# Sixteen dense tokens moved from the dense expert products to gathered rows, with a new start of the program

## What is computed

```python
q = (xb @ w_q).reshape(tb, PEER_HEADS, 2, PEER_HALF)      # 8 heads, 2 halves of 128
sc = jnp.einsum('thjd,hjnd->thjn', q, sub_keys)           # 128 keys in each half
s_half, i_half = lax.top_k(sc, K)                         # K = 16
# 256 sums of pairs; the best 16 name 16 of 128*128 experts for each token and head
idx = jnp.take_along_axis(cand_idx, top_pos, axis=-1)
g = jax.nn.softmax(top_s, axis=-1)
h = jax.nn.gelu(jnp.einsum('td,thkd->thk', xb, u[idx]), approximate=False)
out = jnp.einsum('thk,thkd->td', g * h, v[idx])
```

## Time and profile before

| | us |
|---|---|
| median of 3 runs | 1390.19 (1388.97 to 1390.58) |
| the profiled execution | 1392.18 |
| its span, first to last instruction | 1390.4 |
| TensorE busy | 1367.2 (98%) |
| VectorE busy | 1056.4 (76%) |
| GpSimd busy | 599.5 (43%) |
| ScalarE busy | 438.4 (32%) |
| DMA, mean over the span | 336 GB/s |

### The profile page before, as it was taken

The page is one execution under the profiler, slowest core; times in us unless marked ns, Lnnn a source line. Parts: engine busy times, 40 slices in busy tenths (PEclk is TensorE's granted clock), DMA queues, the critical chain, the costliest instruction groups (busy, mean ns, idle before and its releaser), DMA issues.

```text
span 1390.4 us, 16195 instructions
## 1 busy us (share of the span) xinstructions
PE 1367.2 (98%) x5402; PEld 935.1 (67%) x5402; DVE 1056.4 (76%) x2365; ACT 438.4 (32%) x1219; POOL 599.5 (43%) x516
## 2 busy tenths in 40 slices
PE   7999999999999999999999999999999999999999
PEld 5656648567588888888899999995444444444443
DVE  4535445799899999998589899998768667766665
ACT  2533522444411111113677887882000000000000
POOL 0000001632855554442356655564667745544540
PEclk9999999999999999999999999999999999999999
DMA  8322334985999999996899999999999999999998
GB/s 308 138 108 111 121 125 183 362 314 196 403 389 411 409 352 374 342 350 234 299 377 407 385 398 395 389 382 402 388 410 409 410 409 409 409 409 409 410 409 311
DMA packets 121762, 467.68 MB, mean 336 GB/s; under 512 B 13776, under 2 KB 14160, under 8 KB 115152
## 3 DMA queue, kind: packets, MB, share of 16 engines
q0 software_dynamic: 73728, 268.47, 49.8%
q1 hardware_dynamic: 47664, 197.66, 36.8%
q10 hardware_dynamic: 288, 0.52, 0.1%
HBM read 462.67 MB, written 3.93 MB: 336 GB/s over the span
## 4 chain that ended last, share of the span: by engine, by line
PE 94%; DVE 3%; ACT 2%; issue 1%; DMA 0%; SPq 0%; ACTq 0%; DVEq 0%
PE BANKS L941 32%; PE BANKS L965 32%; PE BANKS L741 11%; PE BANKS L733 10%; PE BANKS L960 4%; PE BANKS L924 1%; PE BANKS L713 1%; PE BANKS L857 1%; PE BANKS L768 1%; PE BANKS L778 0%; DMA BIG<-w_in 0%; PE BANKS L829 0%; DVE NMX L1574 0%; ACT BIG L1122 0%; DVE UV L1638 0%
## 5 line engine op out<-in xcount | busy, mean ns | idle before, releaser
L1685 POOL DMA_INDIRECT UV<-u,IDX x152 | 174.1, 1145 | 398.8 <-DVE IDX L1513 261.2
L1685 POOL DMA_INDIRECT UV<-v,IDX x159 | 191.1, 1202 | 165.9 <-DVE UV L1638 91.3
L1643 DVE SCALAR_TENSOR_TENSOR X<-UV,HG,X 128x1024 f32<-128x1024 f32 x159 | 203.7, 1281 | 39.3 <-DMA UV<-v,IDX 37.1
L941 PE MATMUL BANKS<-T 128*128 128x256 f32 x1024 | 229.2, 379 | 0.0
L965 PE MATMUL BANKS<-T,BIG 128*128 128x512 f32 x512 | 225.2, 592 | 0.0
L965 PE MATMUL BANKS<-Y,BIG 128*128 128x512 f32 x512 | 225.1, 592 | 0.0
L941 PE MATMUL BANKS<-T,Y 128*128 128x256 f32 x992 | 221.9, 379 | 0.0
L1638 DVE SCALAR_TENSOR_TENSOR UV<-UV,Y 128x1024 f32<-128x1024 f32 x152 | 184.9, 1221 | 42.2 <-DMA UV<-u,IDX 40.8
L941 PEld LDWEIGHTS BANKS<-T 128*128 128x128 f32 x1024 | 192.0, 190 | 24.9 <-issue 0.2
L941 PEld LDWEIGHTS BANKS<-T,Y 128*128 128x128 f32 x992 | 186.0, 190 | 24.0
L965 PEld LDWEIGHTS BANKS<-Y,BIG 128*128 128x128 f32 x512 | 97.3, 190 | 122.5 <-issue 122.5
(11 more groups left out here) (258 smaller groups left out, 1222.2 us busy)
## 6 DMA issues: line engine op xcount, KB each, us to landing
T<-u_t SPq DMA_DIRECT2D x64, 512.0 KB
T<-v SPq DMA_DIRECT2D x64, 512.0 KB
Y<-v SPq DMA_DIRECT2D x64, 512.0 KB
Y<-u_t SPq DMA_DIRECT2D x62, 512.0 KB
BIG<-w_in SPq DMA_DIRECT2D x23, 1024.0 KB, 6.7
BIG<-w_q SPq DMA_DIRECT2D x16, 1024.0 KB, 7.4
BIG<-w_out SPq DMA_DIRECT2D x8, 1024.0 KB, 5.9
UV<-v,IDX POOLq DMA_INDIRECT x159
```

The source lines that it names most:

```text
L941: last = nc.tensor.matmul(PS[(i + 2) % 4][:, 0:HT], ub[:, c, :], T8[:, 1, c, :], start=(c == 0), stop=(c == KC - 1))
L1643: stt(xb, row, HG[:, n % 2, i % UNIT:i % UNIT + 1], xb, ALU.mult, ALU.add).then_inc(used, 1)
L1685: pool.indirect_dma_start(row_place(s), None, u if kind == "ru" else v, bass.IndirectOffsetOnAxis(IDX[:, b, c:c + 1], 0)).then_inc(row_in[ ...
```

## The change

16 of the 256 dense tokens (240 to 255 of them, `EXTRA = 16`, `FEW = 240`) no longer go through the dense products of u: `gl` moves 240 columns. Their u products are made from gathered rows, one row for each partition, where the partition stands for a token and a head (16 x 8 = 128) and the row for one of the 16 choices: 16 gathers of 512 KB and 16 VectorE steps `eu`. The steps `xi` find their indices, `ye` spreads their x over the partitions, and `eh` does the Gelu and turns the result; `oh` multiplies it into the maps of the last 4 groups, and `gm` copies there. Their v products stay dense.

The planner is set anew: the due time is 3.36 us for each `gl`, 13 more `ru` and `rv` rows stand in the first u stage (95), and in the second 134 of them and the 16 `eu` (150). 202 rows are left for the v stage; its products are as before.

At the start the loads of x come ahead of the first weights and in two parts instead of three, 12 products of ones by ones go ahead of the first weights' wait, the sum of squares stands before the fourth chunk instead of the fifth, and the step sizes are made in four strips of 32 output rows, which a product with a 0/1 table adds up.

```diff
+STRIP = 32
+EXTRA = P // PH
+FEW = HT - EXTRA
+FEWG = FEW // NTOK
+WARM = 12
...
-            work += [item] + rows(3 - (n >= 13))
+            work += [item] + rows(3)
...
-    work += [first] + on("sel", 0) + rows(9) + on("oh", 0) + [second] + rows(3) + on("oh", 1) + [sums, keys, columns]
-    work += rows(1) + on("ws", 3)
+    work += on("xi", 0) + rows(1) + [first] + on("xi", 1) + on("sel", 0) + rows(9) + on("oh", 0) + [second] + rows(3) + on("oh", 1) + [sums, keys, columns]
+    work += rows(5) + on("ws", 3)
...
-        while w < len(work) and spent < 3.44 * (j + 1):
+        o += on("ye", (j - 4) // 2) if j in (4, 6) else []
+        while w < len(work) and spent < 3.36 * (j + 1):
...
     o += work[w:]
+    o += on("ye", 2)
...
+        o += on("eh", 2) if k == 57 else []
...
-        o += rows(1 + (k % 4 == 0))
+        o += rows(1 + (k % 4 == 0) - (k % 6 == 5))
+        o += extra(1) if k % 3 == 0 and k >= 3 else []
+        if k in (52, 54):
+            o += on("eh", (k - 52) // 2)
...
+            sp.dma_start(T8[:, 0, 0:4], x_t[:, 0, 0:4]).then_inc(ld_t_lower, 16)
             sp.dma_start(COLS[:], cols).then_inc(ld_cols, 16)
-            sp.dma_start(T8[:, 0, 0:2], x_t[:, 0, 0:2]).then_inc(ld_t_first, 16)
+            sp.dma_start(T8[:, 0, 4:8], x_t[:, 0, 4:8]).then_inc(ld_t_upper, 16)
             sp.dma_start(W[:, 0, 0:2 * HALF], tiles[0][0][:, 0:2 * HALF]).then_inc(w_first, 16)
-            sp.dma_start(T8[:, 0, 2:4], x_t[:, 0, 2:4]).then_inc(ld_t[0], 16)
-            sp.dma_start(T8[:, 0, 4:8], x_t[:, 0, 4:8]).then_inc(ld_t_upper, 16)
...
+                pe.wait_ge(ones_set, 1)
+                for k in range(WARM):
+                    nc.tensor.matmul(PS[7][:, 0:P], ONES, ONES, start=True, stop=True)
                 pe.wait_ge(w_first, 16)
-                for c0 in (0, 4):
-                    if c0:
+                for c0, c1 in ((0, 3), (3, 4), (4, KC)):
+                    if c0 == 3:
                         scale_map(0)
...
-                            last = nc.tensor.matmul(bank[0:NH, half * HT:(half + 1) * HT], WDT[:, c * NH:(c + 1) * NH],
-                                                    T8[:, half, c, :], start=(c == 0), stop=(c == KC - 1))
+                            strip = c % 4 * STRIP
+                            last = nc.tensor.matmul(bank[strip:strip + STRIP, half * HT:(half + 1) * HT],
+                                                    WDT[:, c * STRIP:(c + 1) * STRIP], T8[:, half, c, :],
+                                                    start=(c < 4), stop=(c >= 4))
...
-                        last = nc.tensor.matmul(PS[(i + 2) % 4][:, 0:HT], ub[:, c, :], T8[:, 1, c, :],
+                        last = nc.tensor.matmul(PS[(i + 2) % 4][:, 0:FEW], ub[:, c, :], T8[:, 1, c, 0:FEW],
                                                 start=(c == 0), stop=(c == KC - 1))
                     last.then_inc(hd_full, 1)
+                elif step == "ye" and i == 1:
+                    pe.wait_ge(ey_in, 1)
+                    for c in range(KC):
+                        last = nc.tensor.matmul(PS[5 + c // 4][:, c % 4 * P:(c % 4 + 1) * P], X[:, HB, c * P:(c + 1) * P], IDENT,
+                                                start=True, stop=True)
+                    last.then_inc(ye_full, 1)
+                elif step == "xi" and i == 0:
+                    pe.wait_ge(xi_in, 2)
+                    nc.tensor.matmul(PS[7][:, 0:P], ETOK, EALL, start=True, stop=True)\
+                        .then_inc(xi_full, 1)
...
+            def extra_rows(first):
+                if first:
...
+                    stt(EALL, ISELS[:, 1, 1, :], float(NKEY), ISELS[:, 1, 0, :], ALU.mult, ALU.add).then_inc(xi_in, 1)
+                    return
+                dve.wait_ge(xi_full, 1)
+                link(tt(EOWN.rearrange("p (k h) -> p k h", h=PH), PS[7][:, 0:P].rearrange("p (h k) -> p k h", k=TOPK),
+                        bc(OF_HEAD, 1, TOPK), ALU.mult))
+                link(nc.vector.reduce_sum(EIDXF, EOWN.rearrange("p (k h) -> p k h", h=PH), AXX))
+                nc.vector.tensor_copy(EIDX, EIDXF).then_inc(ex_ready, 1)
...
+                elif step == "eu":
...
+                    dve.wait_ge(row_in[k], 16 * fill)
+                    stt(row, row, 1.0, EY, ALU.mult, ALU.mult, accum_out=EH[:, i:i + 1]).then_inc(used, 1)
```

More of the change, by code:

```diff
@@ L111, in rows, with extra @@
         return out
-    place_of_row = lambda: sum(kind in ("ru", "rv") for kind, _ in stream[:place[0]])
+    extra_left = many("eu", 0, EXTRA)
+    def extra(m):
+        out = extra_left[:m]
+        del extra_left[:m]
+        return out
     o = many("x", 0, 4) + on("dt", 0) + many("x", 4, 5) + on("dt", 1) + many("cv", 0, 1) + many("x", 5, 6)
@@ L426, in block_program @@
             if step == "gl":
-                KW[i] = NTOK * done[1]
+                KW[i] = min(NTOK * done[1], FEW)
                 done[0] += 1
@@ L438, in block_program @@
         RAW = {n: m for m, n in enumerate(n for step, n in ORDER if step == "y" and ("e", n) in EXPS)}
+        EH_NEXT = next(i for step, i in ORDER[ORDER.index(("eh", 2)):] if step == "og")
         POS = {s: i for i, s in enumerate(ORDER)}
-        rows_until = lambda step: sum(s[0] in ("ru", "rv") for s in ORDER[:POS[step]])
+        rows_until = lambda step: sum(s[0] in ("ru", "rv", "eu") for s in ORDER[:POS[step]])
         FIRST_V = rows_until(("gm", NGRP - 1))
@@ L1043, in _ @@
                 elif step == "dt" and i == 0:
-                    drain_bank(DTT, view=lambda t: t[0:NH, :])
+                    drain_bank(DTT)
                 elif step == "dt":
@@ L1205, in _ @@
                         last = nc.scalar.activation(bank[:, 0:n], bank[:, 0:n], ACT.Gelu)
-                    if n < HT:
-                        last = nc.scalar.activation(HBUF[:, i, n:HT], bank[:, n:HT], ACT.Gelu)
+                    if n < FEW:
+                        last = nc.scalar.activation(HBUF[:, i, n:FEW], bank[:, n:FEW], ACT.Gelu)
                     last.then_inc(ge_done, 1)
+                elif step == "ye" and i == 0:
+                    nc.scalar.activation(X[:, HB, :].rearrange("p (c t h) -> p c t h", t=EXTRA, h=PH),
+                                         bc(T8[:, 1, :, FEW:HT], 3, PH), ACT.Copy).then_inc(ey_in, 1)
+                elif step == "ye" and i == 2:
+                    act.wait_ge(ye_full, 1)
+                    for c in range(2):
+                        nc.scalar.activation(EY[:, c * FIRSTJ // 2:(c + 1) * FIRSTJ // 2, :],
+                                             PS[5 + c][:, :].rearrange("p (b n) -> p b n", n=EXTRA), ACT.Copy).then_inc(ey_out, 1)
+                elif step == "eh" and i == 0:
+                    act.wait_ge(used, ROWSEQ[("eu", EXTRA - 1)] + 1)
+                    nc.scalar.activation(EH, EH, ACT.Gelu).then_inc(eh_gelu, 1)
+                elif step == "eh" and i == 2:
+                    act.wait_ge(eh_full, 1)
+                    nc.scalar.activation(EHT, PS[4 + EH_NEXT % 4][:, 0:EXTRA], ACT.Copy).then_inc(eh_done, 1)
                 elif step == "gm" and JS[i] < NKEY:
@@ L1630, in _ @@
                     dve.wait_ge(sel_ready, i - HB + 1)
+                elif step == "xi":
+                    extra_rows(i == 0)
+                elif step == "eh" and i == 1:
+                    dve.wait_ge(eh_gelu, 1)
+                    tt(EHM, bc(EH, 1, PH), bc(OF_HEAD, 2, TOPK), ALU.mult).then_inc(eh_in, 1)
+                elif step == "eu":
+                    s = ROWSEQ[(step, i)]
+                    k, fill = PLACES[s][0:2]
+                    row = row_place(s).rearrange("p (b n) -> p b n", n=EXTRA)
+                    if i == 0:
+                        dve.wait_ge(ey_out, 2)
+                    dve.wait_ge(row_in[k], 16 * fill)
+                    stt(row, row, 1.0, EY, ALU.mult, ALU.mult, accum_out=EH[:, i:i + 1]).then_inc(used, 1)
                 elif step in ("ru", "rv"):
@@ L1678, in fetch @@
                     pool.wait_ge(idx_ready, i // UNIT + 1)
+                if kind == "eu" and i == 0:
+                    pool.wait_ge(ex_ready, 1)
                 b, c = i // NSLOT, i % NSLOT
                 k, fill, last_user, _, guard = PLACES[s]
+                at = EIDX[:, i:i + 1] if kind == "eu" else IDX[:, b, c:c + 1]
                 if last_user is not None:
```

86 lines of the change are left out of this document (62 added, 24 removed).

## The result

The changed kernel takes 1407.75 us, the median of 4 runs (1403.95 to 1410.34), beside 1389.91 for the kernel before on the same chips: a ratio of 1.012, 95% interval 1.0102 to 1.0137. It is 17.8 us slower where 4 us faster was forecast, and outside the range of 1377 to 1397. The profiled execution took 1407.91 us, its span is 1406.1.

What follows compares the result with a forecast made beforehand. TensorE held 94% of the chain, with TensorE, VectorE and gathered rows nearly level in the second u stage; 677.8 + 275.5 - 5.5 = 947.8, less 4.6 is 943.2 against 947.5, 4.3 us less: 1386, range 1377 to 1397.

Steps and rivals of the forecast that it cites:

- the 4.6 us of the start: Program start: early x load 2.6 us, strips 1.55 and 0.5 us, together 4.6 us gained (2 to 6).
- start of the v stage, ahead of the last `gw`: Seam to the v stage: TensorE begins it 5.5 us before VectorE's last `gw`, at 947.8 us.
- The step that failed: Second u stage: 147 rows with the DMA at 396 GB/s, the middle between 383 and 409, last 275.5 us.
- The rival with the ring: Second u stage: ring of 5 keeps the rate at 383 GB/s, stage 284.7 us, time 1395; chance 0.27.
- No stretch of this trace comes above 409: Whole trace: 409 GB/s taken as the DMA's most, bounding the second u stage at 266.6 us.
- has room for six more issues: Second u stage: GpSimd, busy 158 of 276 us, can issue six more gathers.
- The end of the first stage: First u stage on VectorE: ends at 677.8 instead of 662.98 us, mainly from 13 more rows costing 15.3 us.
- the wait at `xi` 1: First u stage: VectorE waits 2.5 us (0 to 3.5) for a product standing behind `gl` 59.
- The new wait of TensorE: Seam between the u stages: TensorE waits about 11 us for `oh` 2 from VectorE.
- The chunk products: Program start: products at L733 come near 16.4 instead of 19.04 us, 2.6 us gained (0.5 to 3.5).
- their upper bound: Program start, first half of the step-size products: strips gain 1.55 us, at most 2.6 if four run at once.
- the second half: Program start, later step-size products: they follow VectorE's 8 pieces, so only the tail gains, 0.5 us.

Runs made afterwards that it cites:

- even order: Changed kernel with the same 150 rows of the second u stage laid evenly, never more than 3 to a step instead of up to 4: 1402.67 us, ratio 1.0086.
- half the bytes of u: Changed kernel with the u tiles from 68 on loaded at half width, products using stale data: 1394.18 us, ratio 1.002.
- ring of 4: Changed kernel with 4 places for gathered rows in place of 5: 1448.76 us, ratio 1.0419.
- ten moved: Changed kernel with ten of the second stage's 147 rows moved into the v stage, planner's due time 3.5 us: 1390.27 us, ratio 0.999.
- all but narrow: Changed kernel with `gl` moving 256 columns again, all else kept: 1420.41 us, ratio 1.0225.
- due time 3.5: Changed kernel with the planner's due time of a tile at 3.5 us instead of 3.36: 1403.68 us, ratio 1.0084.
- narrow, 6 rows more: Kernel before with 240 columns in `gl` and six rows moved from the v stage to the second stage: 1386.67 us, ratio 0.9979.
- narrow alone: Kernel before with only `gl` cut to 240 columns, the u products of 16 tokens left out: 1374.20 us, ratio 0.9886.
- sixteen moved: Changed kernel with 16 of the second stage's 147 rows moved into the v stage, planner's due time 3.5 us: 1391.33 us, ratio 1.0005.

## Why the prediction was wrong

Placed side by side (profiled executions, the 4.6 us of the start taken off where the prediction took them off at the end):

| | predicted | measured | off by |
|---|---|---|---|
| `oh` 2 on VectorE | 673.2 | 675.5 | +2.3 |
| second stage | 275.5 | 292.0 | +16.5 |
| start of the v stage, ahead of the last `gw` | 5.5 | 4.9 | +0.6 |
| from there to the end | 444.7 | 445.3 | +0.6 |
| the profiled execution | 1387.9 | 1407.9 | +20.0 |

**The step that failed** is the length of the second stage: "the harder VectorE pulls, the more gathers are under way, and that raises the rate. I take the middle between 383 and 409". How many gathers are under way does not depend on how hard VectorE pulls. In this stage all of them go into the five places of the ring. A place goes round: a gather starts, it lands, the row lies until VectorE comes to it, VectorE works on it, and the next gather into the place starts. Following every row of the stage through the trace gives the mean of each part, in us:

| kernel | start to landing | until VectorE | VectorE's work | until the next gather | the round | by places |
|---|---|---|---|---|---|---|
| after | 7.44 | 0.48 | 1.25 | 0.73 | 9.90 | 1.98 |
| even order | 7.48 | 0.45 | 1.25 | 0.46 | 9.64 | 1.93 |
| half the bytes of u | 6.66 | 0.76 | 1.25 | 0.79 | 9.46 | 1.89 |
| ring of 4 | 6.90 | 0.45 | 1.26 | 0.47 | 9.08 | 2.27 |

The last column, the round divided by the places, is the pace of the rows. The expectation of the ten moved rows adds an issue to the landing of 7.5 us, which has the issue in it already; what the place waits, 1.2 us, is about as long, and so its sum came out right by luck. The second stage by its rows, as measured:

| kernel | rows | stage, us | us per row |
|---|---|---|---|
| after | 147 | 292.0 | 1.99 |
| all but narrow | 147 | 290.7 | 1.98 |
| due time 3.5 | 147 | 291.5 | 1.98 |
| even order | 147 | 285.8 | 1.94 |
| narrow, 6 rows more | 147 | 286.1 | 1.95 |
| narrow alone | 141 | 276.9 | 1.96 |
| ten moved | 137 | 270.9 | 1.98 |
| half the bytes of u | 147 | 279.3 | 1.90 |
| ring of 4 | 147 | 334.8 | 2.28 |

Left out are the kernels with 131 rows and those with 256 columns of before, in which TensorE is busy for all but 2 us of the stage (256.9 of 258.6 with sixteen moved), so that its length says less of the ring. The ring of 4 is the test of it: the round is even shorter than with five places, and the stage longer all the same. No run had six places. Before ran at 276.3 / 141 = 1.96, the same pace, and kept it when its columns were narrowed: TensorE and the ring were level. The number could have been had from the earlier trace rows: 147 rows at 1.96 are 288 us; but TensorE fills that stage of before, and that the ring would go no faster only the narrow kernel showed. The rival with the ring had the right mechanism, but it scaled the stage by bytes, tiles of u included, and so gave 284.7, though it priced a row at 1.9 us, by which six rows more give 287.7. Scaled by rows it gives 288, and the order of after, with up to four rows to a step, about another 6 us by the even order's profile. Its 1395 was 13 us too low.

"No stretch of this trace comes above 409" holds for the stages and not for the start of before, where stretches of 4 us move 426 and 427 GB/s (8 to 12 and 12 to 16 us). The forecast does not hang on it.

**What GpSimd adds.** That GpSimd "has room for six more issues" was right and beside the point. In the second stages of 15 of the kernels the place for the next gather came free, in all cases but one of 2129, only after the gather before it had started: GpSimd was never further behind than that. What it adds is time between a freed place and the next gather. That time has two values (medians): 0.27 us where GpSimd is idle, and 1.12 us where the place comes free less than 1.25 us after the gather before it started. The longer one fell on 72 of 147 gathers in after, 25 of 140 in before, 27 of 148 in the even order and 84 of 147 with half the bytes of u. The 1.4 to 1.9 us of GpSimd's long instructions go with it: of the 64 over 1.3 us in after, 62 are followed by another gather without a pause. From the start of such an instruction to the start of the one behind it are 1.95 us on average, and the one behind it starts 1.12 us after its own place came free; the shortest distance from start to start is 1.24 us. So the long instructions do not show a pace of GpSimd's own. Why the start comes later behind a running gather was not tested.

By the table above the extra wait is worth 0.73 - 0.27 = 0.46 us of each round in after, which over 147 rows in five places is an estimate of 13.5 us of the 292, if nothing else took the time up. The even order saves 0.27 us of it, about all of what its round is shorter. How often the long value falls is not a matter of the order alone, though: with the order of before it fell on 25 gathers, with that order and the new start on 67 of 141.

**The end of the first stage** was right but for 2.3 us. Of the wait at `xi` 1, 3.6 us came where 2.5 stood in the sum (range up to 3.5):

```profile
637.69 0.29 DVE L1620 TENSOR_TENSOR KT<-BANKS,COLS 128x128 f32<-128x128 f32 x1 [3.60 <-PE BANKS L988]
```

With the due time of 3.5 the stage ended 3.1 us earlier, and the ratio fell from 1.012 to 1.0084 (the intervals overlap). The new wait of TensorE, 10.2 us, was expected at 11; the `gl` pace, 3.24 us for 16 instructions, and the v stage were as worked out.

**The start** was sized 4.6 us and divided wrongly. The rows of after against those of the earlier trace rows:

```profile
8.88 5.49 PE L747 MATMUL BANKS<-Y,BIG 128*128 128x256 f32 x12 [3.46 <-DMA BIG<-w_in]
...
15.10 4.48 PE L747 MATMUL BANKS<-Y,BIG 128*128 128x256 f32 x20
19.42 7.07 PE L767 MATMUL BANKS<-T,BIG 128*128 128x256 f32 x32
26.42 1.07 PE L892 MATMUL BANKS<-T,BIG 128*32 128x256 f32 x16
```

The first weights come at 8.88, and the products with them still run at half speed, 458 ns each with a granted clock of 0.50 from 8 to 12 us, though ones by ones stood ahead (they had ended 3.5 us before). The chunk products start at 19.42 instead of 19.04: 0.4 us lost where 2.6 gained stood in the sum. The strips do what their upper bound said: 16 instructions in 1.07 us instead of 3.62, a gain of 2.55 where 1.55 stood; in the second half they gain 0.3 where 0.5 stood. The Trainium skill (TensorEngine Tiling (Array Packing), Theoretical Speedup) gives up to 4x for a small dimension of 32; the trace agrees, with 3.4x. Alone on the chip the strips gain 0.27% (3.7 us), the early load gains nothing (ratio 1.0014, interval 0.9997 to 1.0031), both together 0.1% (0.9978 to 1.0001). The profiled start of the first `gl` scatters by 2 us and more between kernels with the same start (441.8 to 445.8 in four with that of before), so a finer division than this cannot be had from single profiles.

**Where the gain went.** The products save 27.3 us of TensorE; the sixteen tokens ask for 16 gathers of 0.524 MB. At the pace of the second stage these cost 29.5 us there. Where they are moved away from it they meet the v stage, which between 1050 and 1350 us moves 409 GB/s in 14 of the 16 kernels, with 199 to 218 rows to take (415 in the two that add the strips to before): gathers land in it after 24 us instead of 7.5 with sixteen moved, and a row costs 2.06 to 2.08 us. Even at 409 GB/s the 16 gathers are 20.5 us of transfer. From `oh` 2 to the end of the last row the kernels with 349 rows take 707 us (sixteen moved), 712 (ten moved) and 720 (after), before with its 346 rows 709. The 13 other added rows stand in the first stage and lengthened it on VectorE by 15 us. Nothing was left of the 27. The best kernel that gives the whole result is the one with the strips alone, at 1386.91 us: it beats both.

## What to carry to other kernels

When rows come through a ring of a few places, count rows, not bytes: the stage cannot be shorter than rows times (start to landing + use) / places, here 1.75 us a row, and what a place waits for the engines on either side comes on top. The pace measured in the old trace has all of it in it and is the price to take for each row added, here 1.96 us where the consuming engine's work is 1.2 (if another engine fills the old stage, as TensorE did here, the ring alone may be faster, and a run with that engine relieved tells). Before taking columns off a busy engine in exchange for gathers, price the gathers' bytes at the highest rate any stage reaches (16 x 0.524 MB / 409 GB/s = 20.5 us against 27.3 saved): what remains is the most that can be won, and it needs a place to be won in. And a busy share says little of an engine that stands in such a ring: what counts is how soon it answers. Look at the time from a freed place to the next gather's start, and do not take a long record for work before you have looked at what the instruction behind it waits for.

## What the runs showed of the hardware

- An indirect gather of 512 KB occupies GpSimd 0.93 to 1.3 us, and starts 0.27 us after its place is freed where GpSimd is idle. Where the place is freed less than 1.25 us after the start of the gather before, it starts 1.12 us after that (700 of 2129 gathers in the second stages of 15 kernels, medians 1.11 to 1.12 in each), and the gather before is mostly recorded with 1.4 to 1.9 us. The shortest time from start to start is 1.24 us. Why was not tested.
- Four column strips of 32 run at the same time, 3.4 times as fast as one after another: 16 fp32 products of 256 columns in 1.07 us, 67 ns each, against 226.
- Products of ones by ones that end 3.5 us ahead of the first real products left these at 458 ns, twice the 224 ns of the 20 behind them; with none ahead, in before, they took 420. The granted clock in after is 0.50 from 8 to 12 us.
- The landing of a gather, from the start of its instruction (medians), is longer the more is under way: 6.9 us with 4 places, 7.5 with 5, 6.7 with 5 and half the bytes of u, and 24 in the v stage with up to 13 places and 409 GB/s.
